# A first MLP chunk made token-major, and its gate computed as dot products on VectorE

## What is computed

```python
mod_l = (sc_l @ w_mod[i] + b_mod[i])[:, None, :]
sh1_l, s1_l, g1_l, sh2_l, s2_l, g2_l = jnp.split(mod_l, 6, axis=-1)
hl = modulate(rms_norm(xl, norm1_g[i]), sh1_l, s1_l)
yl = conformer_conv(hl, rows, *conv_p)          # ends with silu(...) @ w_pw2 + b_pw2
xl = xl + g1_l * yl
xl = xl + g2_l * sq_relu_mlp(modulate(rms_norm(xl, norm2_g[i]), sh2_l, s2_l),
                             mlp_w1[i], mlp_w2[i])
```

## Time and profile before

| | us |
|---|---|
| median of 3 runs | 1025.73 (1024.15 to 1026.26) |
| the profiled execution | 1025.7 |
| its span, first to last instruction | 1023.8 |
| TensorE matmul busy in the span | 992.0 |
| VectorE busy | 618.1 |
| ScalarE busy | 503.9 |
| mean granted clock of TensorE | 0.993 |

### The profile page before, as it was taken

The page is one execution under the profiler, slowest core; times in us unless marked ns, Lnnn a source line. Parts: engine busy times, 40 slices in busy tenths (PEclk is TensorE's granted clock), DMA queues, the critical chain, the costliest instruction groups (busy, mean ns, idle before and its releaser), DMA issues.

```text
span 1023.8 us, 13497 instructions
## 1 busy us (share of the span) xinstructions
PE 992.0 (97%) x5626; PEld 837.5 (82%) x5626; DVE 618.1 (60%) x748; ACT 503.9 (49%) x628; POOL 25.0 (2%) x47
## 2 busy tenths in 40 slices
PE   8999899999998999999999999999999999999996
PEld 6665689999987999878888888889987788888885
DVE  5786935444448649865455455664895654545465
ACT  4445365455454547644444444653664644443453
POOL 0000000000000000010000000100000100000010
PEclk9999899999999999999999999999999999999999
DMA  9987886654525443245555456435323555555531
GB/s 334 415 307 278 331 349 234 205 200 165 198 70 193 176 152 130 71 165 206 203 170 203 170 200 221 158 133 201 124 83 125 195 206 170 200 186 185 199 110 41
DMA packets 30934, 196.07 MB, mean 192 GB/s; under 512 B 3731, under 2 KB 5832, under 8 KB 9880
## 3 DMA queue, kind: packets, MB, share of 16 engines
q1 hardware_dynamic: 30874, 195.22, 52.6%
HBM read 194.14 MB, written 2.04 MB: 192 GB/s over the span
## 4 chain that ended last, share of the span: by engine, by line
PE 80%; DVE 12%; issue 3%; ACT 3%; DMA 2%; POOL 0%; SPq 0%; DVEq 0%; POOLq 0%; ACTq 0%
PE ps L1652 56%; PE ps L2007 9%; PE ps L2063 5%; DVE lo L1068 3%; ACT hi L612 1%; DMA scratch<-stream 1%; PE ps L1757 1%; PE ps L2311 1%; PE ps L2193 1%; PE ps L2147 1%; DVE scratch L1444 1%; DMA h<-x 1%; DVE scratch L1510 1%; DVE scratch L1461 1%; PE ps L2214 0%
## 5 line engine op out<-in xcount | busy, mean ns | idle before, releaser
L1068 DVE TENSOR_TENSOR lo<-raw,hi 128x2048 fp32r<-128x2048 f32 (+5 forms) x140 | 310.3, 2219 | 232.1 <-ACT hi L612 232.1
L612 ACT ACTIVATE hi<-raw 128x2048 fp32r<-128x2048 f32 (+4 forms) x140 | 263.8, 1888 | 143.1 <-PE ps L1652 110.1
L1652 PE MATMUL ps<-hi,xh 128*128 128x512 f32 (+2 forms) x704 | 275.1, 391 | 10.0 <-DVE xl L1109 4.4
L1652 PE MATMUL ps<-lo,xh 128*128 128x512 f32 (+2 forms) x704 | 269.2, 382 | 0.0
L1652 PE MATMUL ps<-hi,xl 128*128 128x512 f32 (+2 forms) x704 | 268.9, 382 | 0.0
L1652 PEld LDWEIGHTS ps<-hi,xh 128*128 128x128 f32 x704 | 132.2, 188 | 45.0 <-issue 11.1
L1652 PEld LDWEIGHTS ps<-lo,xh 128*128 128x128 f32 x704 | 132.1, 188 | 25.1
L1652 PEld LDWEIGHTS ps<-hi,xl 128*128 128x128 f32 x704 | 132.4, 188 | 22.6
L1652 PE MATMUL ps<-hi,gh 128*128 128x512 f32 (+2 forms) x328 | 125.2, 382 | 0.0
L1652 PE MATMUL ps<-lo,gh 128*128 128x512 f32 (+2 forms) x328 | 124.6, 380 | 0.0
L1652 PE MATMUL ps<-hi,gl 128*128 128x512 f32 (+2 forms) x328 | 124.5, 380 | 0.0
(11 more groups left out here) (257 smaller groups left out, 1062.8 us busy)
## 6 DMA issues: line engine op xcount, KB each, us to landing
raw<-stream SPq DMA_DIRECT2D x142, 1024.0 KB, 4.8
scratch<-stream SPq DMA_DIRECT2D x22, 1024.0 KB, 8.9
raw<-stream SPq DMA_DIRECT2D x4, 1020.0 KB, 5.0
raw<-stream SPq DMA_DIRECT2D x4, 896.0 KB, 4.9
raw<-stream SPq DMA_DIRECT2D x2, 864.0 KB, 4.5
raw<-stream SPq DMA_DIRECT2D x2, 768.0 KB, 5.1
raw<-stream SPq DMA_DIRECT2D x2, 680.0 KB, 5.1
h<-x SPq DMA_DIRECT2D x2, 512.0 KB, 5.3
```

What stands on the lines that cost most here:

```text
L612: nc.scalar.activation(hi[:, u["s"] % SPLIT_SLOTS, 0:n], raw_of(u, n), ACT.Copy).then_inc(S["hi_done"], 1)
L1068: nc.vector.tensor_tensor(lo[:, slot, first:n], raw_of(u, n)[:, first:n], hi[:, slot, first:n].bitcast(F32), ALU.subtract).then_inc(S["lo_ ...
L1652: ins = nc.tensor.matmul(out, l, r, start=start and i == 0, stop=stop and i == 2, skip_group_check=skip)
```

## The change

The last gate (v = 5) joins `DOTS`: its four units are used by DVE instead of PE. In the stream they move from ahead of w1 chunk 1 into the MLP: the unit (5, j-1) stands between w1 of chunk j and w2 of chunk j-1, for j = 1 to 4. DVE does its two dot products at the end of its work for chunk j, and after the fourth the gate column, which goes to DRAM and back (`gate_row(1)`) ahead of the loads of w1 chunk 7. PE's quarters 8 to 11 and the row sums go, with ACT's copies of them.

PE does the last two units of pw2 with `closing_pair`: block 0's first 512 columns over both units, its second 512, then block 1 over the first unit, then block 1's first 512 columns of the last unit, the transposes of block 0, and the rest. w1 of chunk 0 becomes token-major: tokens stationary, 512 columns streaming, block 0 over both units, the transposes of block 1, block 1 over both units. The hidden layer of chunk 0 is therefore not transposed; eight transposes (`first_hidden_T`) follow between the two units of w1 chunk 1.

DVE and ACT work on the blocks in turn: residual of block 0, low half of w1 part 1, normalisation of block 0, and so on; ACT squares in halves of 512, and it squares block 0 ahead of the high half of w1 part 1. The shift and scale are 128 columns wide; ACT does features 0 to 3 and DVE features 4 to 7.

```diff
-DOTS = {(0, 0), (0, 1), (0, 2), (0, 3), (2, 0), (2, 1), (2, 2), (2, 3), (4, 2), (3, 2), (4, 3), (3, 3)}
+DOTS = {(0, 0), (0, 1), (0, 2), (0, 3), (2, 0), (2, 1), (2, 2), (2, 3), (4, 2), (3, 2), (4, 3), (3, 3), (5, 0), (5, 1), (5, 2), (5, 3)}
...
     add("w1", 0, [4, 4], MLP_CHUNK)
-    mod(5, 0, 1, 2, 3)
     for j in range(MLP_CHUNKS + 1):
         if 0 < j < MLP_CHUNKS:
             add("w1", j, [4, 4], MLP_CHUNK)
+        if 0 < j <= GROUPS:
+            mod(5, j - 1)
         if j:
             add("w2", j - 1, [2, 2], D)
...
+            def gate_row(g, dst):
+
+                sp.wait_ge(S["gate_done"], g + 1)
+                sp.dma_start(gate_dram[g].rearrange("(p j) -> p j", p=P), one["gate"][:, g * KT:(g + 1) * KT]).then_inc(S["gate_dma"], 16)
+                sp.wait_ge(S["wave_ps"], CHUNKS)
+                sp.wait_ge(S["gate_dma"], 32 * g + 16)
+                sp.dma_start(dst, gate_dram[g].partition_broadcast(P)).then_inc(S["gate_dma"], 16)
...
+            at, end = end, units_of("w1", 7)[0]["index"]
+            weights(UNITS[at:end])
+            gate_row(1, gate2)
...
+            def mid_squares(b):
+
+                for c in range(2):
+                    if c == 0:
+                        act.wait_ge(S["res_step"], 3 * b + 2)
+                    else:
+                        act.wait_ge(S["h_ready"], hval(1, b))
+                    cs = slice(c * CHUNK, (c + 1) * CHUNK)
+                    nc.scalar.activation(xs[:, b, cs], h[:, b, cs], ACT.Square, scale=D ** -0.5,
+                                         accum_out=half_ss[:, 2 * b + c:2 * b + c + 1]).then_inc(S["sumsq"], 1)
+
+            def mid_high(b):
+
+                act.wait_ge(S["midT_ps"], b + 1)
+                if b == 0:
+                    act.wait_ge(S["used"], last_of("pw2")["s"] + 1)
...
+                sl = slice(b * P, (b + 1) * P)
+                for i in range(KT // 2):
+                    pair = slice(2 * i, 2 * i + 2)
+                    if i < 2:
+                        for f in (2 * i, 2 * i + 1):
+                            nc.scalar.activation(full[:, f, sl], ps[:, 4 + 2 * b, f * P:(f + 1) * P], ACT.Identity, scale=in_scale[:, KT + f:KT + f + 1],
+                                                 bias=in_shift[:, KT + f:KT + f + 1]).then_inc(S["mid_own"], 1)
+                        act.wait_ge(S["mid_own"], 4 * b + 2 * (i + 1))
+                    else:
+                        act.wait_ge(S["mid_full"], 4 * b + 2 * (i - 1))
+                    nc.scalar.activation(xh[:, pair, sl], full[:, pair, sl], ACT.Copy).then_inc(S["mid_hi"], 1)
+
+            mid_squares(0)
             feed(units_of("w1", 0)[1], 0)
...
+            mid_high(0)
+            mid_squares(1)
+            mid_high(1)
...
+            dve.wait_ge(S["gate_dma"], 32)
+            mid_residual(0, 0)
+            mid_residual(0, 1)
+            feed(units_of("w1", 0)[1], 0)
+            mid_norm(0)
+            mid_residual(1, 0)
+            dve.wait_ge(S["scale_done"], 2 * GROUPS)
+            dve.wait_ge(S["shift_done"], 2 * GROUPS)
+            mid_second(0)
+            mid_low(0, 0, 1)
+            mid_residual(1, 1)
+            mid_low(0, 2, 3)
+            mid_norm(1)
+            mid_second(1)
+            mid_low(1, 0, 1, 2, 3)
...
+                if 0 < j <= GROUPS:
+                    dots(5, j - 1)
+                if j == GROUPS:
+                    gate_column(1)
...
-            token_major(units_of("pw2")[0:3], xh, xl, halves, lambda b, i: ps[:, 2 * b + i, :], opened=True, waits=pw2_waits, closed=False)
-            for b in range(NB):
-                last_pw2(b)
-            pe.wait_ge(S["res_step"], 3)
-            quarters(8)
-            row_sum(0)
-            next_quarters(9)
+            token_major(units_of("pw2")[0:2], xh, xl, halves, lambda b, i: ps[:, 2 * b + i, :], opened=True, waits=pw2_waits, closed=False)
+            pe.wait_ge(S["yl_done"], KT // 2)
             pe.wait_ge(S["shift_done"], 6)
-            mid_T(0)
-            row_sum(1)
-            next_quarters(10)
-            mid_T(1)
-            row_sum(2)
-            next_quarters(11)
+            closing_pair(units_of("pw2")[2:4], xh, xl, lambda ins: ins.then_inc(S["pw2_ps"], 1), KT - 1, lambda: mid_T(0))
...
+            def mid_waits(u, b):
+
+                pe.wait_ge(S["mid_lo"], 4 * b + 2 * u["part"] + 2)
+
+            def second_mid_T(u, b):
+
+                if u["part"] == 0 and b == 1:
+                    mid_T(1)
+
+            token_major(units_of("w1", 0), xh, xl, [slice(0, MLP_CHUNK)], lambda b, i: ps[:, b, :],
+                        done=lambda ins: ins.then_inc(S["w1_ps"], 1), waits=mid_waits, together=(2,), between=second_mid_T)
...
-                    if j == 0 and u["part"] == 1:
-                        row_sum(3)
+                    if j == 1 and u["part"] == 1:
+                        first_hidden_T()
```

More of the change, by code:

```diff
@@ L324, in build @@
         sq = one["yb"][:, 0:KT * SEQ].rearrange("p (f t) -> p f t", f=KT)
+        full = one["u"].rearrange("p (k t) -> p k t", k=KT)
         hid1 = one["yb"][:, 0:NB * MLP_CHUNK].rearrange("p (b c) -> p b c", b=NB)
@@ L424, in stage_free @@
                 return
[L425 to L429, removed]
+            eng.wait_ge(S["col_sums"], [m - 4 in g for g in COLUMN_UNITS].index(True) + 1)
         NORMS = 3 + 3 * LAYERS + 1
@@ L551, in _ @@
             weights(UNITS[at:end])
[L552 to L556, removed]
+            gate_row(0, one["g1"])
             at, end = end, units_of("w1", 1)[0]["index"]
@@ L1325, in _, with mid_residual @@
-            for b in range(NB):
-                if b:
-                    feed(units_of("w1", 0)[1], 0)
+            def mid_residual(b, c):
+                at = 2 * b + c
+                if at < 3:
+                    dve.wait_ge(S["pw2_ps"], at + 1)
+                else:
+                    product(dve, "pw2")
+                cs = slice(c * CHUNK, (c + 1) * CHUNK)
+                nc.vector.tensor_tensor(xs[:, b, cs], ps[:, at, :], one["g1"][:, cs], ALU.mult).then_inc(S["res_step"], 1)
+                rstep[0] += 1
+                dve.wait_ge(S["res_step"], rstep[0])
+                ins = nc.vector.tensor_tensor(h[:, b, cs], xs[:, b, cs], h[:, b, cs], ALU.add)
+                if c == 0:
+                    ins.then_inc(S["res_step"], 1)
+                    rstep[0] += 1
+                else:
+                    ins.then_inc(S["h_ready"], 1)
@@ new lines, in mid_low @@
+            def mid_low(b, *pairs):
+                sl = slice(b * P, (b + 1) * P)
+                for i in pairs:
+                    dve.wait_ge(S["mid_full"], 4 * (b + 1))
+                    dve.wait_ge(S["mid_hi"], KT // 2 * b + i + 1)
+                    pair = slice(2 * i, 2 * i + 2)
+                    nc.vector.tensor_tensor(xl[:, pair, sl], full[:, pair, sl], xh[:, pair, sl].bitcast(F32), ALU.subtract).then_inc(S["mid_lo"], 1)
+            dve.wait_ge(S["gate_dma"], 32)
+            mid_residual(0, 0)
@@ L1688, in token_major, with closing_pair @@
                                 used(ins, u)
-            def closing_pair(units, ah, al, finished, k_last):
+            def closing_pair(units, ah, al, finished, k_last, before_last=None):
                 first, last = units
@@ L1725, in closing_pair @@
                         finished(ins)
+                        if before_last:
+                            before_last()
                 used(ins, last)
@@ L1936, in pw2_waits @@
                     column_sums(5)
-            def last_pw2(b):
-                u = last_of("pw2")
-                pw2_waits(u, b)
-                wh, wl = parts(u)
-                sl = slice(b * P, (b + 1) * P)
-                for i, c in enumerate(halves):
-                    for k in range(u["kts"]):
-                        kk = u["k0"] + k
-                        ins = three(ps[:, 2 * b + i, :], xh[:, kk, sl], xl[:, kk, sl], wh[:, k, c], wl[:, k, c], start=False,
-                                    stop=kk == KT - 1)
-                    ins.then_inc(S["pw2_ps"] if 2 * b + i < 3 else S["used"], 1)
             def mid_T(b):
@@ L1989, in w2_product @@
                     used(ins, u)
-            for j in range(MLP_CHUNKS):
+            for j in range(1, MLP_CHUNKS):
                 if j >= 2:
```

139 lines of the change are left out of this document (53 added, 86 removed).

## The result

| | before | after |
|---|---|---|
| median, us | 1024.94 (1023.47 to 1026.26, 4 runs) | 1043.26 (1040.62 to 1044.80, 4 runs) |
| profiled execution | 1025.7 | 1043.56 |
| its span | 1023.8 | 1041.8 |
| mean granted clock | 0.993 | 0.984 |

The changed kernel is slower: ratio 1.0176, 95% interval 1.015 to 1.0203. Forecast were 1038.3 us and a range of 1029.6 to 1047. The time grew by 17.9 us between the profiled executions, where 12.6 were forecast.

What follows compares the result with a forecast made beforehand. TensorE, busy for 97% of the span, was taken as the bound. 1025.7 + 4.6 (transition chain) + 2.0 (clock) + 6.0 (MLP stalls) = 1038.3 us, with an 8-in-10 range of 1029.6 to 1047.

Steps and rivals of the forecast that it cites:

- The start of block 0's chain: Before w1 of chunk 0: first residual still at 120.31, block 0's transposes at 128.7 after 9.6 us of TensorE idling.
- The conversion and the two open gaps: After each of the two groups of mid transposes: shift-and-scale and copies leave TensorE idle 3.0 us before w1 products.
- +4.6 for the chain: Transition up to w2 of chunk 0: its start comes at 164.0 instead of 159.43, before any clock loss.
- The stalls in the MLP: w2 of chunks 1 to 3: loads wait for slots held by the dot products; TensorE idles 2.0 us each, +6.0.
- T + 13.5: T is the end of w2 of chunk j-1; the next w2 could start 13.5 us later, though wanted at T+11.51.
- the 4.4 set beside it: Landing time of a one MB load by the skill's DMA fit, instead of 4.8; stall 1.6, MLP part 4.8.
- The clock: Transition: idling lowers TensorE's clock for one low stretch, two thirds on w1 matmuls; +2.0 taken, from 0 to 6.6.
- rival B: Clock falls in every gap, MLP stalls too, each of five costing up to 3.3; 1046 us with three; chance 13%.
- A: MLP loads are covered after all, by a misread slot or order; only 6.6 remain, 1032.3 us; chance 14%.
- C: Transition: block overlap works through an earlier residual for block 0, w2 at 152.0; faster, 1021.9 us; chance 8%.
- D: No change: conversion takes 2.0, clock stays full (+0.3), MLP loads are covered; 1026.0 us; chance 6%.
- What costs nothing: Dropped sel tile, gain_row(2), and gate_row(1)'s round trip before w1 chunk 7, covered by the ring; rest keeps its length.

Runs made afterwards that it cites:

- the norm first: The changed kernel with ScalarE's high half of w1 chunk 0 part 1 ahead of block 0's squares, VectorE's low half behind block 0's normalisation: 1039.62 us, ratio 1.0143.

## Why the prediction was right, and where it was not

**The start of block 0's chain: right.** Finishing block 0 early bought nothing. VectorE's first residual stands at 120.19, by the load that ScalarE waits for the earlier trace rows. The transposes of block 0 came at 128.53 where 128.7 was forecast, with 9.40 us of idling where 9.6 was.

**The conversion and the two open gaps: right.** 3.16 and 3.02 for the forecast 3.0, the shift-and-scale pair at 0.82 and 0.70 to 0.71, the copy at 0.42. (The 3.1 that the prediction sets beside its 3.0 fits as well.) Of the +4.6 for the chain, 3.3 is left when the low clock in w1 is taken out: the first product was at 135.55 instead of 136.5, because eight transposes and six matmuls at the low clock ended sooner than I had them, and small groups took 0.89 instead of 1.04.

**The stalls in the MLP: right.** Forecast T + 13.5 in three rounds, measured T + 13.50, 13.46 and 13.47; +6.0 forecast, +5.9 measured. The fourth round has none. Moving the dots took them away, with nothing else changed. The three loads landed 4.80, 4.75 and 4.76 us after their release, by the row and not by the 4.4 set beside it; SP issues them, not the GpSimd path that the section cited there is about. Two small slips: the terms as written add up to T + 13.4, and the 0.02 us of issue between the links are the rest; and eight dots at 1.22 and 0.08 would be 10.4 in all, but neighbours overlap, and the chain has 2.30 for each unit's two, the 9.2 that was written.

**The clock: the term that was mis-sized.** I took +2.0, one low stretch, and called it a choice. It was 5.05 in the transition, because w1 ran at the low clock behind both gaps of 3 us, within the 0 to 6.6 that stood there, and 3.9 in the MLP, which the forecast had at nothing. 8.9 against 2.0 accounts for more than the 5.3 us by which the profiled execution is above the forecast; the chain, 1.3 cheaper than forecast, gave part of it back. The step that failed is the one that weighed rival B: "the stalls are shorter". They were, 2.0 us against the 2.3 to 2.5 of the earlier trace rows, and two of the three were followed by a loss of 1.8 us, the middle one by 0.2. So rival B had the mechanism. Its price of 3.3 a gap was too high: the five gaps cost 3.16, 1.89, 1.82, 0.22 and 1.83. Filled with work, the pieces behind them cost 0.2 to 0.3 more than the warm price, which is the direct test. So the number is right by the stated range, and not by the forecast's own: 1043.26 lies just above the 1034 to 1043 that the main forecast gave itself, and nearer to B's 1046 than to 1038.3.

**The rivals.** A (loads covered) falls with the stalls. C (faster, the blocks overlap) falls with the first residual, which didn't move. With the feeds out of the chain, the clock held and the dots early, the overlap of the blocks comes to 1025.1: even then it gains nothing that can be measured. D falls too: the conversion took 3.0 to 3.2 and the loads were not covered.

**What costs nothing: right.** The starts of w1 of chunk 7 are 18.15 us apart and the spans 18.0, so the rest of the kernel has its old length, and the round trip of the gate's row ahead of w1 chunk 7 costs nothing.

Left open: why the middle stall lost only 0.2 us. It is as long as the other two by the chain. It isn't the place either: with the dots late, the cheap stall is the second of three in the changed kernel (0.22), the first where the gate moved alone (0.07) and the third with the norm first (0.22), and the other six lost 1.8 to 1.9 each. One gap of 3.0 us, with the norm first, cost only 0.26 more as well. So a gap's length alone doesn't decide whether a low stretch follows; what does, no run here shows, and no run varied the length of a gap finely. With one profiled execution of each kernel, 5.05 and 3.9 are what these gaps cost in one execution, not a fixed price.

## What to carry to other kernels

With a ring of slots, ask of each user when it lets its slot go, and count from there to the use of the load behind it: release, landing, split. A consumer that is idle for most of a round can still hold up everything if it uses its operand last; moving eight operations a few lines up was worth 10 us here.

Work taken from the busiest engine gives nothing at a place where that engine waits for a chain on others. It can lose there, because the work had held the clock up. Price each new gap on TensorE twice: its length, and what the matmuls behind it may lose at the low clock (1.8 to 3.2 us in four of the five gaps here, next to nothing in the other). Take the price of a filler from a trace before choosing its count.

## What the runs showed of the hardware that was not expected

**A short stall can lower TensorE's clock.** Gaps of 2.0 us in a stream that was else without a break were followed by matmuls at 1.2 GHz, at a loss of 1.8 to 1.9 us each, in two of three in each of three kernels. The level doesn't fall in the gap: it is 0.94 from 192 to 193 and 1.00 from 243 to 244, where the matmuls have resumed, and 0.50 and 0.54 in the microsecond after. Behind the middle stall it stays at 1.00 (218 to 221).

**A long two-input operation of VectorE holds up GpSimd.** A GpSimd operation of one element a partition took 1.64 us beside VectorE's 2048-column subtraction and 0.19 when that was moved away. It did so in the kernel before as well. The Trainium skill, page "GPSIMD Engine Reference", section "1. Specifications", says that GpSimd shares its SBUF interfaces with VectorE and contends with VectorE instructions that have two SBUF inputs. The runs agree, and show that the small operation may wait for nearly all the rest of the long one: it ended 0.04 us after it.

**A plain fp32 product of 128 columns on constants is two instructions** in the trace and costs 0.223 us in a stream, nearly as much as one 512-column matmul of the split products (0.227).
